# Gated linear attention in two passes of one head pair, laid between half of the gate products

## The reference, cut to what matters

```
h = rms_norm(x, g_mix);  proj = h @ w_in        # q,k,v of attention; lq,lk,lv,lr,laf,lab of GLA; gate_a, gate_l
o_attn = gqa_attention(aq, ak, av) @ w_attn_up  # 8 query heads, 2 kv heads, head size 64, softmax over all keys
# GLA, 4 heads, dk 64, dv 128, chunks of 64 tokens, forward and backward:
g = log_sigmoid(a @ w + b) / 16                 # low-rank gate, one per direction
b = cumsum(g) within a chunk
A[t,s] = sum_d q[t,d] k[s,d] exp(b[t,d] - b[s,d])
o = A v + (q exp(b)) S;  S = exp(b_last) S + (k exp(b_last - b))^T v
o = rms_norm(o_f + o_b, gla_norm) * silu(lr)
merged = sigmoid(gate_a) * o_attn + sigmoid(gate_l) * (o @ w_gla_up)
x = x + merged @ w_out;  x = x + expert_choice_ffn(...);  x = x + ple(...)
```

## Time and profile before

| | us |
|---|---|
| median of 3 runs | 2738.11 (2737.79 to 2738.43) |
| the profiled execution | 2737.88 |
| its span, first to last instruction | 2736.3 |
| PE busy | 2341.1 (86%) |
| DVE, ACT, POOL busy | 939.3, 631.6, 354.1 |

### The profile page before, as it was taken

One profiled execution on the slowest core, in us unless ns is written; L12 is line 12 of the kernel. 1 busy time (PEld: TensorE's weight loads), 2 busy tenths in 40 slices (PEclk: granted clock), 3 DMA queues, 4 the chain that ended last, 5 costly groups with the idle time before them and its releaser, 6 DMA issues. The chain is left out here.

```text
span 2736.3 us, 34885 instructions
## 1 busy us (share of the span) xinstructions
PE 2341.1 (86%) x14370; PEld 2060.0 (75%) x14370; DVE 939.3 (34%) x1532; ACT 631.6 (23%) x1103; POOL 354.1 (13%) x306
## 2 busy tenths in 40 slices
PE   5987959999998347976998649999999999999598
PEld 5986836666665135855888539999999999999476
DVE  4205543343333687045343651111111111111454
ACT  4211222323231322014333101111111111111344
POOL 0121111111110384010000000001100011000000
PEclk9998979999999566558998769999999999999799
DMA  4213211111111200026242056776676766765211
GB/s 137 84 56 112 95 48 40 44 42 46 40 44 54 77 1 1 0 73 220 93 142 96 31 223 246 248 250 236 222 263 230 255 234 236 250 226 186 77 69 67
DMA packets 175490, 348.37 MB, mean 127 GB/s; under 512 B 14384, under 2 KB 52656, under 8 KB 173104
## 3 DMA queue, kind: packets, MB, share of 16 engines
q1 hardware_dynamic: 156832, 283.37, 29.1%
q0 software_dynamic: 18576, 63.85, 7.4%
HBM read 292.78 MB, written 54.39 MB: 127 GB/s over the span
## 5 line engine op out<-in xcount | busy, mean ns | idle before, releaser
L1757 PE MATMUL ps<-e_x,e_raw 128*128 128x160 f32 x4096 | 560.6, 299 | 0.0
L1757 PEld LDWEIGHTS ps<-e_x,e_raw 128*128 128x128 f32 x4096 | 559.3, 190 | 0.6
L1757 PE MATMUL ps<-e_h,e_raw 128*128 128x160 f32 x2048 | 298.3, 300 | 0.0
L1757 PEld LDWEIGHTS ps<-e_h,e_raw 128*128 128x128 f32 x2048 | 281.5, 190 | 1.8
L828 DVE TENSOR_REDUCE a_nmax<-ps 128x1 f32<-128x1024 f32 (+1 forms) x80 | 84.9, 1061 | 197.5 <-PE ps L762 197.2
L1843 ACT ACTIVATE aff_hidden<-ps 128x160 f32<-128x160 f32 x128 | 38.9, 304 | 472.9 <-PE ps L1757 472.9
L795 PE MATMUL ps<-a_p,v_ones 128*128 128x512 f32 (+1 forms) x288 | 146.2, 590 | 0.0
L154 PE MATMUL ps<-act_hi,w_hi 128*128 128x512 f32 (+1 forms) x384 | 141.7, 369 | 0.0
L1863 DVE TENSOR_TENSOR aff_hidden<-ps,aff_hidden 128x160 f32<-128x160 f32 x128 | 41.6, 325 | 287.9 <-ACT aff_hidden L1843 287.9
L1871 DVE TENSOR_SCALAR e_y_s<-ps,gate_s 128x256 f32<-128x256 f32 x64 | 30.9, 483 | 307.3 <-PE ps L1797 307.3
L155 PE MATMUL ps<-act_lo,w_hi 128*128 128x512 f32 (+1 forms) x384 | 136.3, 355 | 0.0
(11 more groups left out here) (289 smaller groups left out, 4353.5 us busy)
## 6 DMA issues: line engine op xcount, KB each, us to landing
e_raw<-in_w_gate_e SPq DMA_DIRECT2D x32, 2048.0 KB, 7.6
e_raw<-in_w_up_e SPq DMA_DIRECT2D x32, 2048.0 KB, 10.7
e_raw<-in_w_down_e SPq DMA_DIRECT2D x32, 2048.0 KB, 7.6
w_raw<-in_w_blk SPq DMA_DIRECT2D x18, 1024.0 KB, 5.0
early<-fm_scratch SPq DMA_DIRECT2D x80, 128.0 KB, 3.7
fm_scratch<-a_fm_out POOLq DMA_DIRECT2D x32, 256.0 KB, 2.3
tm_scratch<-tm_out POOLq DMA_DIRECT2D x50, 128.0 KB, 2.0
fm_scratch<-fm_out POOLq DMA_DIRECT2D x9, 640.0 KB, 3.2
```

What stands on the lines that cost most here:

```text
L1757: last = pe.matmul(ps[:, bank, 0:CAP], raw[slot][:, k, cols], src[:, k, :], start=(k == 0), stop=(k == KT - 1))
```

## The change

It does four things.

**Gate products.** Attention keeps four of the eight gate blocks: a tile of 128 columns per head, so three groups of 24 products in place of six, at steps 7, 12 and 17 (the first group of head 0 comes ahead of its row maxima). The other eight tiles go to GLA, through a new class that loads, rounds and subtracts tiles of 128 columns; there DVE takes the low half. The first block of attention is now split at the end of the rope stage.

**Attention's order.** The sample units come first and the prompt last, and the row maxima are spread anew: one after each of steps 3 to 6 and 13 to 16, and both of the prompt at step 12, with the row of the prompt behind them.

**GLA in two passes.** Each pass does one pair of heads from the logits to the stored output. One walk gives the order for all engines; between its parts stand calls `fill(w)`, each of which puts a share of the 192 gate pieces (three products each) in PE's list. The weights sum to 202 over both passes. Where the last piece of a group falls in a `fill`, ACT's copy of that group, and the work on the next tile, stand at that place in the other lists. POOL does no arithmetic any more: both differences and both multiplies of a level are on DVE, one pair wide.

**Token-major outputs.** The output products now have tokens on the partitions. ACT squares them, DVE sums over the features, takes the root's inverse and scales, PE transposes the result back, and DVE applies gain and silu(r). The products with ones are gone. The weights' first piece for the merge is loaded at the end of GLA, into the common raw buffer.

```diff
+GATES_BEFORE_GLA = 4
...
+            split(nth(TM_BLOCKS + MID_BLOCKS))
...
-        UNITS = [(N_SAMPLE, N_PROMPT, NT_S, NT)] + [(c, Q, 0, NT_S) for c in range(0, N_SAMPLE, Q)]
+        UNITS = [(c, Q, 0, NT_S) for c in range(0, N_SAMPLE, Q)] + [(N_SAMPLE, N_PROMPT, NT_S, NT)]
...
-        group_at = {s: g for g, s in enumerate((3, 6, 9, 11, 14, 17))}
...
+        this_head = {3: [4], 4: [5], 5: [6], 6: [7], 12: [8, 9]}
+        next_head = {13: [0], 14: [1], 15: [2], 16: [3]}
+        row_at = {first_of[1] - 1: 1, 12: 2}
+        NEXT_ROW = NS - 1
...
+        group_at = {first_of[1] - 1: 0, 12: 1, NS - 1: 2}
...
+        def walk(fill, loads=skip, prelude=skip, spread=skip, level=skip, tail=skip, state_step=skip, out=skip, close=skip):
+
+            for hp in range(GLA_HP):
+                loads(hp, 0)
+                fill(4 if hp else 10)
+                for d in range(2):
+                    prelude(hp, d)
+                    fill(5)
+                for d in range(2):
+                    spread(hp, d)
+                    fill(6)
+                for l in range(NL):
+                    level(hp, l)
+                    fill(6)
+                level(hp, NL)
+                fill(3)
+                for d in range(2):
+                    tail(hp, d)
+                    fill(3)
+                loads(hp, 1)
+                for n in range(len(batches)):
+                    state_step(hp, n)
+                    fill(2)
+                loads(hp, 2)
+                fill(2)
+                for n in range(TWOS + 1):
+                    if n < TWOS:
+                        out(hp, n)
+                        fill(2)
+                    if n:
+                        close(hp, n - 1)
+                        fill(1)
...
+            def fill(w):
+                at[0] += w
+                upto = len(todo) * at[0] // sum(weights)
+                for m, g, kk in todo[at[1]:upto]:
+                    piece(m, g, kk)
+                    if kk == KT - 1:
+                        group(m, g)
+                at[1] = upto
...
+            def level(hp, l):
...
+                for n, (a0, a1) in enumerate(QUADS):
+                    if l:
+                        pe.wait_ge(S["lvl_read"], 2 * ((hp * (NL + 1) + l - 1) * NQ + n + 1))
+                    for a in range(a0, a1):
+                        for par in range(2):
+                            rows = slice(par * DK, (par + 1) * DK)
+                            last = pe.matmul(lvl_bank(par, n)[:, a - a0, :], kk[rows, pairs(a)], qq[rows, pairs(a)], start=True, stop=True)
+                    last.then_inc(S["lvl_mm"], 1)
...
+            def out(hp, n):
...
+                    for par in range(2):
+                        pe.matmul(o[:, par, pair, :], att[:, a, par, :], v[:, a, par * DV:(par + 1) * DV], start=True, stop=False,
+                                  skip_group_check=True)
+                    for d in range(2):
+                        for j in range(2):
+                            c = 2 * (2 * n + pair) + j
+                            if c in FIRSTS[d]:
+                                continue
+                            for par in range(2):
+                                rows = slice(par * DK, (par + 1) * DK)
+                                last = pe.matmul(o[j * CHUNK:(j + 1) * CHUNK, par, pair, :],
+                                                 (kl if d else ql)[1][rows, c * CHUNK:(c + 1) * CHUNK], state[d][rows, c, :],
+                                                 start=False, stop=True, skip_group_check=True)
...
+            def piece(m, g, kk):
+                b, use = m % 2, m * G + g
+                if (g, kk) == (0, 0):
+                    tiles.ready(pe, m)
+                if kk == 0 and use >= 2:
+                    pe.wait_ge(S["g_read"], use - 1)
+                first, width = CHUNKS_512[g]
+                x = [a[:, kk, first:first + width] for a in (ah, al)]
+                w = [a[:, kk, :] for a in (tiles.hi[b], tiles.lo[b])]
+                last = split3(pe, ps[:, G_BANK + use % 2, 0:width], w, x, kk == 0, kk == KT - 1)
+                if kk == KT - 1:
+                    last.then_inc(tiles.used[b] if g == G - 1 else S["g_done"], 1)
+
+            walk(filler(piece=piece), prelude=prelude, level=level, tail=tail, state_step=state_step, out=out, close=close)
 
         @block.scalar
...
+            def out(hp, n):
+                use = hp * TWOS + n
+                act.wait_ge(S["out_mm"], use + 1)
+                act.wait_ge(S["ss_done"], use)
+                act.wait_ge(S["r_silu"], hp + 1)
+                act.activation(sq, out_bank(n), ACT.Square).then_inc(S["sq_done"], 1)
+                act.wait_ge(S["ms_done"], use + 1)
+                act.activation(stat[:, n % 2, 2, :], stat[:, n % 2, 1, :], ACT.Sqrt).then_inc(S["rt_done"], 1)
+
+            def group(m, g):
+                use = m * G + g
+                group_done(act, m, g)
+                act.wait_ge(fm_stored, 16 * use)
+                first, w = CHUNKS_512[g]
+                act.activation(fm_out[:, 0:w], ps[:, G_BANK + use % 2, 0:w], ACT.Copy).then_inc(S["g_read"], 1)
+                if g == 0 and m + 1 < tiles.count:
+                    tiles.high(act, m + 1)
+
+            tiles.high(act, 0)
+            walk(filler(group=group), prelude=prelude, spread=spread, level=level, tail=tail, loads=loads, out=out)
...
+            def level(hp, l):
...
+                dve.tensor_tensor(ql[l % 2], ql[l % 2], q[:, :], ALU.mult).then_inc(S["lvl_turn"], 1)
+                dve.tensor_tensor(kl[l % 2], kl[l % 2], k[:, :], ALU.mult).then_inc(S["lvl_turn"], 1)
+                differ(hp, l + 1)
+                gather(hp, l)
+
...
+            def out(hp, n):
+                use, b = hp * TWOS + n, n % 2
+                s = lambda i: stat[:, b, i, :]
+                dve.wait_ge(S["sq_done"], use + 1)
+                dve.tensor_reduce(s(0), sq.rearrange("p h a c -> p (h a) c"), AX.X, ALU.add).then_inc(S["ss_done"], 1)
+                dve.wait_ge(S["ss_done"], use + 1)
+                dve.tensor_scalar(s(1), s(0), 1.0 / DV, EPS, ALU.mult, ALU.add).then_inc(S["ms_done"], 1)
+                dve.wait_ge(S["rt_done"], use + 1)
+                chain.turn(use)
+                chain.link(dve, dve.reciprocal(s(3), s(2)))
+                newton(dve, chain, s(3), s(1), s(2))
+                if n >= 2:
+                    dve.wait_ge(S["t_mm"], use - 1)
+                rs = s(3).rearrange("p (h a) -> p h a", h=2).unsqueeze(3).broadcast_to((P, 2, 2, DV))
+                dve.tensor_tensor(scaled[b], out_bank(n), rs, ALU.mult).then_inc(S["out_read"], 1)
+
+            def close(hp, n):
+                cols = slice(2 * n * P, (2 * n + 2) * P)
+                dve.wait_ge(S["t_mm"], hp * TWOS + n + 1)
+                dve.wait_ge(S["r_silu"], hp + 1)
+                dve.scalar_tensor_tensor(r[:, :, cols], turned(n), gain[:, 0:1], r[:, :, cols], ALU.mult, ALU.mult).then_inc(S["final"], 1)
...
-                seam = blocks(bb, m)[:, :, m:m + 1].broadcast_to((P, FLAT // (2 * m), 2 * m))
-                pool.tensor_tensor(blocks(diff[1], m), blocks(bb, m), seam, ALU.subtract).then_inc(S["lvl_db"], 1)
-                pool.wait_ge(S["lvl_exp"], l + 1)
-                pool.tensor_tensor(flat(kl[l % 2]), flat(kl[l % 2]), flat(k), ALU.mult).then_inc(S["lvl_k"], 1)
```

More of the change, by code:

```diff
@@ L672, in walk @@
             build(0)
-            for m in range(len(EARLY)):
+            group(0, 0)
+            for m in row_tiles[0]:
                 largest(0, m)
@@ new lines, in stage_gla @@
+        q, k = sb("g_q", [P, T]), sb("g_k", [P, T])
+        bcum = sb("g_b", [P, 2, T])
+        both = sb("g_diff", [P, 2, T])
+        turns = sb("g_turn", [P, 2, 2, T])
+        att = sb("g_att", [P, PAIRS, 2, P])
+        state = [sb(f"g_state{d}", [P, NCH, DV]) for d in range(2)]
+        v = sb("g_v", [P, PAIRS, 2 * DV])
+        mask = sb("g_mask", [P, NL + 1, P], I32)
+        fm_out = sb("g_fm_out", [P, 512])
+        tiles.place(mem)
+        w_lora = sb("g_w_lora", [2 * LORA, 2, GLA_HP, P])
@@ new lines, in stage_gla @@
+        decay = sb("g_decay", [P, 2, NCH])
+        gain = sb("g_gain", [P, 1])
+        bias = sb("g_bias", [P, 2, GLA_HP])
+        stat = sb("g_stat", [P, 2, 4, 4])
+        diff = [both[:, d, :] for d in range(2)]
+        ql, kl = ([turns[:, b, n, :] for b in range(2)] for n in range(2))
+        lora = both[0:2 * LORA, 0, :]
+        z = [turns[:, 0, d, :] for d in range(2)]
+        lg = [turns[:, 1, d, :] for d in range(2)]
+        reset = state[1][:, :, :].rearrange("p c d -> p (c d)")[:, 0:T + 1]
@@ new lines, in stage_gla, with state_place @@
+        batches = [[(d, c) for n in range(at, at + BATCH) for d, c in ((0, n), (1, NCH - 1 - n)) if c not in ENDS[d]]
+                   for at in range(0, NCH, BATCH)]
+        BUFS = 3
+        STATES = NCH - 2
+        order = [[c for s in batches for e, c in s if e == d] for d in range(2)]
```

(51 more changed lines are left out.)

714 lines of the change are left out of this document (342 added, 372 removed).

## The result

The changed kernel takes 2603.3 us (median of 4 runs, 2599.6 to 2604.6) against 2738.3: a ratio of 0.950 (0.949 to 0.951). 2623 was forecast, with a range of 2570 to 2680. The profiled execution has a span of 2602.8 us, 133.5 less than before.

What follows compares the result with a forecast made beforehand. PE was taken to bound attention (94% busy), while GLA mostly runs one engine at a time. From 2737.9 us, less 94.6 for attention and 21.9 for GLA, plus 1.5 for the handover, came 2623 us, range 2570 to 2680.

Steps and rivals of the forecast that it cites:

- Attention, -94.6 forecast: First score to last value product: 483.7 us falls to 389.1, with heads of 49.9 us (47.2 to 53.3) in place of 61.04.
- the 3.4 us behind the query copies: Attention: PE's existing wait per head for the row maxima behind ACT's query copies, 3.4 us, was taken to stay.
- 2.7 for the prompt's chain and the rows: Attention, new waits per head: 1.7 us for step 12's chain of prompt maxima and row, 0.5 for each of two other rows.
- Rival 2: Attention follows a chain and not PE: heads of 53.3 us, a little more in GLA, 2650 us in all; 10%.
- GLA, -21.9 forecast: GLA's two passes, 167.5 and 158 us, take 325.5 us together in place of 347.4.
- 10.0 + 1.2x: GLA level where a gate group ends: chain in us, x the gate pieces up to that end; 1.05 more if ACT rounds.
- 5.5 per step forecast: GLA outputs: each step 5.5 us, between 4.6 at full and 8.8 at half clock; 30 us per pass (25 to 50).
- Rival 1: Half clock in GLA's states and outputs: outputs 8.8 us per step instead of 5.5, 2670 us in all; 18%.
- Rival 3, copies free: Group copies cost nothing in GLA: levels at 9.0 save 32 us, heads at 47.2 save 22, 2569 us in all; 9%.
- Rival 4: PE bound all through GLA at half clock, small tiles not overlapping: GLA 506 us, 2803 us in all, slower; 4%.
- Mode changes: PE draining when tiling mode changes, some 44 runs of small tiles: estimated 19 us of PE, sum some 10 higher, nothing added.
- Handover, +1.5 forecast: GLA to merge: first split waits some 2 us longer, its first x arrives no sooner, so 1.5 us more (0 to 5).

Runs made afterwards that it cites:

- second experiment: The changed kernel, but in GLA ACT copies a finished gate group out, and rounds the next tile, behind the next level's four exponentials: 2564.9 us (0.936).
- Experiment 1: The changed kernel, but attention keeps all eight gate blocks, six groups per head, and GLA has no gate pieces: 2641.5 us (0.965).
- experiment 10: The kernel before, but output products of a pair's two heads alternate in one run, using both row halves of PE: 2703.7 us in one run.
- experiment 5: The changed kernel, but the merge's first 1 MB of weights is loaded ahead of the last three stores of GLA: 2599.4 us (0.949).
- experiment 4: The kernel before, old attention order, but three of the six groups of gate products per head left out: 2653.9 us in one run.

## Why the prediction was right, and where not

The profiled execution took 2604.6 us, 18.3 less than the sum of the forecast. Attention is 13.4 of them, GLA with the seam ahead of it 7.6 and the time up to the first score 3.1; the handover (3.8) and the end (1.9) go the other way.

- **Attention, -94.6 forecast, -108.0 measured: the largest miss.** The step that failed is the waits: I kept the 3.4 us behind the query copies and added 2.7 for the prompt's chain and the rows, 6.1 per head. In five heads the trace has 20.1 us, 4.0 each. Both terms were too large: the old wait is 2.0 to 2.6 us, 2.3 on average, and the new ones are 1.7, of which 1.1 is the prompt's chain. Why the old wait became shorter is not shown. Heads take 48.1 us (240.48 / 5), not 49.9, and 8 x 1.8 = 14.4 us is the whole difference. Rival 2, 53.3 per head, is refuted; my own bounds give 47.2 + 3.4 + 1.0 = 51.6 and not 53.3.
- **GLA, -21.9 forecast.** From its first instruction (769.2) it takes 319.5 us; 325.5 was forecast. Pass by pass: up to the first level 40.0 and 33.1 (40 and 31); five levels 59.3 and 63.4 (59 and 63); sixth level and tail 28.5 and 21.5 (23.5 and 20.5); states 13.9 and 10.6 (15 and 13.5); outputs 23.1 and 26.1 (30 and 30). The sum of five levels came out to within half a us, and the second experiment shows that the cause, ACT's order, was the right one. But single levels (13.8, 14.1, 8.7, 9.1, 13.5, and 15.4, 8.8, 10.2, 12.3, 16.7) differ from what the forecast gives for each, 9.0 or 10.0 + 1.2x and the rounding, by 1.5 us less to 1.0 us more; that the sums are so close is in part luck. The first tail was 5 us longer. I had charged 3 us for the group end ahead of its exponentials; it cost 4.9, since that level took 13.7 in place of 8.8 (ACT's copy stands at 880.42, and DVE, done at 878.5, goes on at 882.2). Another 2.0 lie behind the key multiplies, where the transposes and the pieces among them ran at clock 0.60 and in the second pass at 1.00. The last 1.0 the second tail has too. The 6.0 us of the whole are errors of both signs: outputs 10.8 and states 4.0 too long in the forecast, tails 6.0, preludes 2.1 and levels 0.7 too short.
- **The outputs** were mis-sized: 5.5 per step forecast, 4.0 and 4.6 measured (23.1 and 26.1, less 2.9 for silu, over five). That is about the 4.6 at full clock, without the 0.9 that I had put on it; from the first to the fifth reduction (L1396) PE is busy for 14.58 of 15.19 us and for 17.46 of 17.46, so the sum of its products is what sets the step. Experiment 1 shows them to be the main gain of the new GLA, which the prediction did not say, since it set only the whole of GLA against the whole.
- **Rival 1, half clock in states and outputs**, is refuted by the clock of 0.98 to 1.00. Even in experiment 1, without pieces, only the first step and a part of the second were at half clock, and the outputs took 23.4 us, since the later steps, 3.4 us each, were shorter. So the reason I gave for full clock, the dense pieces between, was not needed, and why the old outputs stayed at 0.50 is not shown. Its price had a slip: 2.6 at full clock are 5.2 at half, not 4.8, so some 0.4 more per step.
- **Rival 3, copies free**, did not happen, but the second experiment made it happen: the ten levels took 32.8 us less there, where 32 were forecast, and all of GLA 38.0 less.
- **Rival 4** rested on 0.236 us for each of the products of L1055. That price was real but belonged to one tile with eight instructions, not to small products as such (experiment 10).
- **Mode changes.** I added nothing for them. The outputs took no longer than the bare sum, so the runs give no reason to add it. The 0.22 us was idle time of the weight loads; the products of the same line had none.
- **Handover, +1.5 forecast, +5.3 measured.** The step that failed is "its first x arrives no sooner": SP's own first issue came later, since the stage waited for the last gate group's store, behind the 1 MB (experiment 5). The sum had no term for that store.

## What to carry to other kernels

Work that is laid into another stage costs little by its products and much by the small instructions that must follow them: put each of these behind the work that the other stage waits for, on every engine's list. Price a small product by what its tile has to do, and see that both row halves and both column halves are in use before blaming the clock. And split a gain by stages of equal work before and after: here the largest part of it, 98.9 of 133.5 us, came from the outputs, not from what the change was named for.

## What the runs showed of the hardware

- Different tiles of PE work beside each other whatever the order in the list: 0.67 and 0.69 us for 16 instructions in two orders, and 1.97 for 8 on one tile or 16 on two.
- PE busy for 102.75 of 102.80 us stayed at clock 0.50 throughout, while the outputs after ran at 0.98 to 1.00. In experiment 1, without pieces between, they were at 0.50 in the first step and at 1.00 from the third on. What makes the difference, no run here shows.
- Two waits of PE of 1.54 and 2.35 us close together were followed by some 5 us at half clock (experiment 4). In the changed kernel the wait behind the query copies stands alone: four heads, with 2.0 to 2.5 us of it, ran at 1.00, and the fifth, with 2.62 us, had some 3 us at half clock and 0.97 over the head.
- A store of 128 KB landed 5.6 us after its issue when a load of 1 MB had been issued 0.3 us ahead of it, and after 2.0 us when not (experiment 5).
